# RWKV stage of a one-core block: heads of token half 1 turned one unit earlier, the next norm's weights in a place of their own, the fourth input unit in another PSUM bank

## The reference

```
x = layer_norm(ALPHA * x + 0.5 * swiglu_2(x, ...), ln_g[0, 0], ln_b[0, 0])      # norm "rw"
proj = x @ rwkv_w_in                                # 2816 columns = 11 units of 256
mix = rwkv7_mix(proj[..., :RWKV_SHIFT], ...)        # token shift, decays, chunked recurrence
heads = concatenate([mix, memory_attention(proj[..., RWKV_SHIFT:], mem_k, mem_v)])
x = layer_norm(ALPHA * x + heads @ w_out[0], ln_g[0, 1], ln_b[0, 1])            # norm "f4"
x = layer_norm(ALPHA * x + 0.5 * swiglu_2(x, ...), ln_g[0, 2], ln_b[0, 2])      # FFN 4

def layer_norm(x, g, b):
    mu = mean(x); var = mean((x - mu) ** 2)
    return (x - mu) * rsqrt(var + 1e-5) * g + b

# at the end of rwkv7_mix
    out = ((out - m) * rsqrt(var + 64e-5)) * lnx_g + lnx_b
    y = (out + bonus) * g
```

## Time and profile before

| | us |
|---|---|
| median of 3 runs | 1703.74 (1703.65 to 1704.11) |
| the profiled execution | 1700.73 |
| its span | 1699.4 |
| PE busy | 1639.3 (96%) |
| DVE busy | 942.3 (55%) |
| ACT busy | 802.6 (47%) |
| POOL busy | 129.6 (8%) |

### The profile page before, as it was taken

How to read it: one execution, slowest core, us unless ns; L and a number is a source line. 1 busy time by engine, 2 the same in 40 slices (tenths; PEclk the granted TensorE clock), 3 DMA queues, 4 the chain that set the end, 5 groups by cost and what they waited for, 6 DMA issues and landing times.

```text
span 1699.4 us, 29823 instructions
## 1 busy us (share of the span) xinstructions
PE 1639.3 (96%) x13094; PEld 1503.6 (88%) x13094; DVE 942.3 (55%) x1199; ACT 802.6 (47%) x1059; POOL 129.6 (8%) x117
## 2 busy tenths in 40 slices
PE   7999999988999999999999989999999999999998
PEld 7999897767999989998998879998999988789997
DVE  6444463445545555445795565546645474575545
ACT  6444444434444454444655254444544456764443
POOL 0000020000000001000376101000020010001000
PEclk9999999879999999999999999999999999999999
DMA  7745443313655445554530066454655542345551
GB/s 275 270 176 195 153 174 150 123 50 125 215 185 188 169 169 203 183 189 149 179 124 4 3 223 223 174 198 149 225 179 193 180 169 98 125 174 199 191 181 75
DMA packets 40865, 280.67 MB, mean 165 GB/s; under 512 B 4794, under 2 KB 4794, under 8 KB 8864
## 3 DMA queue, kind: packets, MB, share of 16 engines
q1 hardware_dynamic: 39024, 272.40, 44.6%
q0 software_dynamic: 1712, 6.37, 1.0%
HBM read 277.14 MB, written 1.08 MB: 164 GB/s over the span
## 4 chain that ended last, share of the span: by engine, by line
PE 90%; DVE 4%; ACT 3%; DMA 2%; issue 1%; SPq 0%; DVEq 0%; ACTq 0%
PE P L231 88%; PE P L242 2%; DMA raw<-ws 1%; ACT whi L205 1%; DMA gb<-gains 1%; DVE wlo L219 1%; DVE xt L279 1%; ACT xt L272 0%; DVE x L359 0%; PE P L2011 0%; DVE AR L791 0%; ACT AR L817 0%; DVE AR L371 0%; DVE AR L1077 0%; DVE AR L2120 0%
## 5 line engine op out<-in xcount | busy, mean ns | idle before, releaser
L231 PE MATMUL P<-xt,whi 128*128 128x256 f32 x5088 | 934.5, 286 | 14.6 <-DVE xt L279 12.1
L231 PEld LDWEIGHTS P<-xt,whi 128*128 128x128 f32 x5088 | 803.8, 193 | 29.3 <-issue 18.3
L231 PE MATMUL P<-xt,wlo 128*128 128x256 f32 x2544 | 702.3, 283 | 0.0
L219 DVE TENSOR_TENSOR wlo<-raw,whi 128x2048 fp32r<-128x2048 f32 x245 | 559.7, 2290 | 80.8 <-PE P L231 76.9
L205 ACT ACTIVATE whi<-raw 128x2048 fp32r<-128x2048 f32 x245 | 467.1, 1908 | 161.2 <-PE P L231 120.2
L231 PEld LDWEIGHTS P<-xt,wlo 128*128 128x128 f32 x2544 | 488.7, 192 | 0.0
L653 DVE TENSOR_TENSOR AR<-P,AR 128x256 f32<-128x256 f32 x114 | 48.4, 425 | 334.6 <-ACT AR L624 334.6
L624 ACT ACTIVATE AR<-P 128x256 f32<-128x256 f32 x114 | 43.7, 384 | 354.3 <-PE P L231 354.3
L231 PE MATMUL P<-whi,hh 128*128 128x512 f32 x504 | 197.5, 392 | 0.0
L231 PE MATMUL P<-wlo,hh 128*128 128x512 f32 x504 | 196.8, 390 | 0.0
L231 PE MATMUL P<-whi,hl 128*128 128x512 f32 x504 | 196.1, 389 | 0.0
(11 more groups left out here) (225 smaller groups left out, 934.8 us busy)
## 6 DMA issues: line engine op xcount, KB each, us to landing
raw<-ws SPq DMA_DIRECT2D x249, 1024.0 KB, 4.8
gb<-gains SPq DMA_DIRECT2D x16, 512.0 KB, 7.3
AR<-by_distance POOLq DMA_DIRECT2D x1, 3072.0 KB, 19.5
x<-x_in SPq DMA_DIRECT2D x2, 512.0 KB, 4.0
AR<-mem_in POOLq DMA_DIRECT2D x1, 1024.0 KB, 5.2
out<-x SPq DMA_DIRECT2D x2, 512.0 KB, 2.6
cs<-cst SPq DMA_DIRECT2D x1, 737.0 KB, 14.1
AR<-cst POOLq DMA_DIRECT2D x1, 420.0 KB, 4.6
```

Of the source, the lines that this page charges most:

```text
L219: dve.e.tensor_tensor(k.wlo[n % NLO][:, :], k.raw[u % NRAW][:, :], k.whi[n % NHI][:, :].bitcast(F32), ALU.subtract).then_inc(*k.s_lo.inc(u))
L231: return pe.e.matmul(o, l, r, start=start, stop=stop, skip_group_check=True)
```

## The change

It does five things.

1. `RW_PROJ`: unit U+3 goes to bank 6 instead of 3, U+5 to bank 7, U+6 to bank 6. PE's wait for `s_tt` of the lead unit U+1 ahead of U+3 goes. The waits of two bonus sums swap with their banks.
2. ACT's splits of the next units in the lead (`hi_to`) stand behind the cross copy of the next lead unit instead of ahead of it.
3. `heads_tensor(1)` stands ahead of half 0 of the third unit (U+14) instead of behind it.
4. The gains of norm f4 go to 2048 columns of the big work tile AR from column 3072 (the token-wise v and k of the stage lay there), and their load waits for `s_pe "read" 1`, the last reading of these, instead of for the heads.
5. SP's order around F0 is: gains, F1, F0, F2 instead of F0, gains, F1, F2.

```
+def gains_tile(k, name):
+    return ar(k, 3072, 2048, "p (a n) -> p a n", a=2) if name == "f4" else k.gb

 def load_gains(k, q, name, rows):
-        q.e.dma_start(k.gb[:, j, :], src).then_inc(*k.s_gn[j].inc(name, by=16))
+        q.e.dma_start(gains_tile(k, name)[:, j, :], src).then_inc(*k.s_gn[j].inc(name, by=16))

 (LayerNorm.rest_vector: in1=k.gb[:, 0, c] and k.gb[:, 1, c] become gains_tile(k, t)[:, 0, c] and [:, 1, c])

-RW_PROJ = {..., 3: (3, "LT", 18), 4: (0, "R", 0), 5: (6, "R", 2),
-           6: (7, "R", 4), ...}
+RW_PROJ = {..., 3: (6, "LT", 18), 4: (0, "R", 0), 5: (7, "R", 2),
+           6: (6, "R", 4), ...}

 (rwkv_inputs_tensor)
-    pe.wait_ge(*k.s_tt.after("rw", 1, 1))
-    cols_tensor(k, pe, U + 3, 3)
+    cols_tensor(k, pe, U + 3, 6)
...
-    cols_tensor(k, pe, U + 5, 6)
+    cols_tensor(k, pe, U + 5, 7)
     low_rank(1)
-    cols_tensor(k, pe, U + 6, 7)
+    cols_tensor(k, pe, U + 6, 6)

 (rwkv_inputs_scalar)
     for n in range(3):
         lead_scalar(k, act, "rw", U + n, n, k.rw_cross[n])
+        hi_to(k, act, U + n + 3)
         shifted_scalar(k, act, n)
         squares(2 * n)
         squares(2 * n + 1)
-        hi_to(k, act, U + n + 4)
+    hi_to(k, act, U + 6)

 (bonus_tensor)
-    pe.wait_ge(*(k.s_ev.after("kk", 5), k.s_ev.after("z", 3), k.s_ev.after("z", 5))[n])
+    pe.wait_ge(*(k.s_ev.after("kk", 5), k.s_ev.after("z", 5), k.s_ev.after("z", 3))[n])

 (rwkv_out_tensor)
     for u, n in units:
+        if n == 2:
+            heads_tensor(k, pe, 1)
         last = out_tensor(k, pe, u, n, False, 0)
     last.then_inc(*k.s_dn.inc("rw", "out"))
-    heads_tensor(k, pe, 1)

 (sync_program)
-    load_units(k, sp, U_FFN3 + 6, U_RWKV + 16)
-    gains("f4", (6, 7), [k.s_ev.after("heads", 1, 1)])
-    load_units(k, sp, U_RWKV + 16, U_FFN4 + 6)
+    load_units(k, sp, U_FFN3 + 6, U_RWKV + 15)
+    gains("f4", (6, 7), [k.s_pe.after("read", 1)])
+    load_units(k, sp, U_RWKV + 16, U_RWKV + 17)
+    load_units(k, sp, U_RWKV + 15, U_RWKV + 16)
+    load_units(k, sp, U_RWKV + 17, U_FFN4 + 6)
```

More of the change, by code:

```diff
@@ L371, in rest_vector @@
             dve.e.scalar_tensor_tensor(out=k.XC[:, a, c], in0=k.x[:, a, c], scalar=sm[:, 8 + a:9 + a],
-                                       in1=k.gb[:, 0, c], op0=ALU.add, op1=ALU.mult).then_inc(*k.s_dv.inc(t, "centred", a, h))
+                                       in1=gains_tile(k, t)[:, 0, c], op0=ALU.add, op1=ALU.mult).then_inc(*k.s_dv.inc(t, "centred", a, h))
         dve.wait_ge(*k.s_sq.after(t, a))
@@ L382, in rest_vector @@
             dve.e.scalar_tensor_tensor(out=k.x[:, a, c], in0=k.XC[:, a, c], scalar=sm[:, 10 + a:11 + a],
-                                       in1=k.gb[:, 1, c], op0=ALU.mult, op1=ALU.add).then_inc(*k.s_xn.inc(t, a, h))
+                                       in1=gains_tile(k, t)[:, 1, c], op0=ALU.mult, op1=ALU.add).then_inc(*k.s_xn.inc(t, a, h))
     def scalar(self, act, a):
@@ L1447, in wide @@
     return t.unsqueeze(2).to_broadcast([128, 12, 64])
-RW_PROJ = {0: (0, "K", 6), 1: (1, "K", 8), 2: (2, "K", 10), 3: (3, "LT", 18), 4: (0, "R", 0), 5: (6, "R", 2),
-           6: (7, "R", 4), 7: (0, "VT", 12), 8: (1, "VT", 14), 9: (2, "VT", 16)}
+RW_PROJ = {0: (0, "K", 6), 1: (1, "K", 8), 2: (2, "K", 10), 3: (6, "LT", 18), 4: (0, "R", 0), 5: (7, "R", 2),
+           6: (6, "R", 4), 7: (0, "VT", 12), 8: (1, "VT", 14), 9: (2, "VT", 16)}
 LOW_BANKS, BONUS_BANKS, QUERY_BANK = (4, 5), (3, 6, 7), 5
```

## The result

| | before | after |
|---|---|---|
| median of the timed runs, us | 1703.32 (20 runs, 1699.96 to 1707.33) | 1698.0 (20 runs, 1693.17 to 1703.08) |
| ratio of the times | | 0.9971 [0.9963, 0.998] |
| the profiled execution, us | 1700.73 | 1699.7 |
| its span, us | 1699.4 | 1698.4 |

The change makes the kernel faster by 0.29%: by the ratio 4.9 us, by its interval 3.4 to 6.3. Forecast were 1700.3 us and a gain of 3.47. The sign was right. The size was too small.

What follows compares the result with a forecast made beforehand. PE, busy 96% of the span, was taken as the bound, losing time only standing still or at half clock. Gains of 0.32 + 2.7 + 0.45 = 3.47 us took 1703.74 to 1700.3 us, range 1698.4 to 1702.2.

Steps and rivals of the forecast that it cites:

- rival D: Slower through PE's clock: extra half-clock bursts in input units, FFN 4's lead and long products, 1707.7 us; chance 0.03.
- Rival C: Moving half 1's heads does not reach norm f4, F0 lands no sooner: only 0.8 us gained, 1702.9 us; chance 0.08.
- The dip in half 1: Half clock within half 1 after PE stood 3.11 us: should vanish, counting for nothing in the sum.
- The dip in the lead: Half clock in F0's lead ahead of FFN 4, on the path: kept at its price of 1.5 us.
- rival B: The dip in FFN 4's lead grows: 1.5 us given back, 2.0 us gain remains, 1701.7 us; chance 0.19.
- Rival A: The dip ahead of FFN 4 goes or falls into PE's gap: 5.0 us gained in all, 1698.7 us; chance 0.20.
- The price of 1.5 us: Cost of half clock in F0's lead: 28 matmuls took 5.10 us there, 3.61 us at full clock.

Runs made afterwards that it cites:

- the filling: Full change plus three matmuls on constants, result overwritten, in PE's stand ahead of FFN 4's lead: 1696.35 us, ratio to the kernel before 0.9948.
- L388 first: Full change with ACT's split of F0 in norm f4 moved behind L388 of half 0: 1695.1 us, ratio 0.9943; run again 1693.54 us, 0.9948.

## Why the prediction was right and where it was not

**Edits 1 and 2: the term that failed.** The forecast was "Gain 0.32 us, and not more, since PE then ran without a stop for 59.84 us", with bounds of 0 and 0.32. The wait and its cause were read rightly. Two things were not.

First, the 0.32 is the idle time from the modelled end of one matmul to the start of the next. PE's start times say 0.47 and 0.64 in the two profiles of before shown above, and at equal clock (with a dip on both sides) the stage falls from 74.63 to 74.80 down to 74.04 to 74.14, that is by 0.5 to 0.75 us.

Second, "PE then ran without a stop" holds, but it ran a part of it at half clock. The dip near 840 us costs 1.5 us (74.1 against 72.56). It stands in all six profiles of kernels without edits 1 and 2, and in three of the ten with one or both. I had the dips on either side of the norm in my sum and looked for none here; the price was in no bound of the range either. Only rival D named dips in the input units, and as a loss.

Is that chance? The bare count is weak: the thought came up after six of these profiles, and of the ten taken later the dip is in three of three without the edits and in two of seven with them, which chance alone gives in 21 of 252 ways. The clock earlier in the same execution says more. Here are two profiles of one and the same kernel, the full change. The third of them, without a dip near 840, has one near 611 us, where nothing is edited; the first, with a dip near 840, has none there (windows, columns as above):

```profile
611.30:614.70 3.40, 3.40 (x18) 3.40 (x18) 0.08 (x1) 1.20 (x1) 0.00 (x0) 0.51 0.04 14
```

```profile
608.00:620.00 12.00, 9.78 (x81) 9.37 (x80) 3.01 (x6) 6.38 (x7) 0.00 (x0) 1.00 0.45 169
```

Sorted by that dip, all sixteen profiles fall into place. In the eleven that have it, the dip near 840 stands in four of four without edits 1 and 2 and in none of seven with one or both (chance: 1 in 330 ways). In the five that don't have it, the dip near 840 is always there, with the edits (three) and without (two). Read so, the edits take the dip away in the executions of the first kind and do nothing to it in the second. If eleven in sixteen is the share of the first kind, that is 0.7 dips an execution, 1.05 us, and the whole term is about 1.6. The sorting was found by looking at these same traces, and no run was made to try it.

The timed runs neither show this size nor rule it out. Edits 1 and 2 together have 1.0 us by the ratio, edit 1 alone -0.2 and edit 2 alone 0.5, each with an interval 3 to 4 us wide; the mean granted clocks of their runs, 0.9794, 0.9793 and 0.9794, against 0.9787, 0.9795 and 0.9795 in their runs of before, show no common rise.

Why the edits change the clock stays open. The matmuls in front of the dip are the same, with the same beat. In before they read:

```profile
836.24 2.85 PE L231 MATMUL P<-AR 12*128 12x256 f32 x12
839.03 1.14 PE L231 MATMUL P<-AR,gb 64*128 64x256 f32 x8
```

and the edits only bring them half a microsecond forward. No run took these thin matmuls away or filled them up.

**Edit 3** was right: forecast 2.7 us, and the stage fell by 2.70 to 2.75 in each of the eight profiles with it. PE's gap ahead of half 1 was to shrink from 3.11 to about 0.4 and is 0.38. The transposes were forecast near 975.3 and stand at 976.77, which is no fault of the term: the second reading was 1.18 us later in this execution. The claim that the path over F0 moves along also holds. Behind the second reading the split of F0 starts 19.12 us later in after and 21.91 in before, 2.8 us less. Rival C (the move doesn't reach the norm, 1702.9) falls with that, and with edit 3 alone measured at 2.9 us.

**Edits 4 and 5** were right: L374 waits for L388 instead of L371, the stage falls by 0.5 us (three profiles of before and those with other edits 12.9 to 13.5, six with the gains in their own place 12.55 to 12.73), where the forecast was 0.45. The 6.53 us of DMA in the chain were worth about a twelfth of their length, since the path over F0 ended only 0.5 us sooner. The gains, issued at 965.27, are waited for by nothing.

**The clock.** The dip in half 1 was to go at no gain, and it went: the windows 978 to 992 are at 1.00, and half 1's first matmul (980.70) and the next turn (988.99) lie 8.29 us apart, forecast 8.2. Over all profiles half 1 has half clock in the eight without edit 3, where PE stood 3.11 or 3.12 us ahead of it, and in none of the eight with it, where it stood 0.38.

The dip in the lead was kept, and two of three profiles of the full change have it as before (6.07, 6.05; 6.06 before). The stand ahead of it was forecast as 4 us and is 2.85 against 2.01. The profiled execution after has the longer dip, 6.90. That is rival B for one execution, with 0.84 of its 1.5 us. Rival A (the dip goes, 1698.7) is near the measured median, and would be the wrong reason for it: no profile of the full change lacks the dip. It took the filling, or L388 first, to remove it there.

The price of 1.5 us was read wrongly for the kernel before. Its second profile has no half clock in the lead, and from the first L359 of norm f4 to the second turn it takes 19.26 us, against 19.20 and 18.96 with it: without the dip PE stands for the norm of half 1. In the changed kernel that norm is done sooner, and there the dip is paid for: 18.61 and 18.72 us with it (19.57 with the longer one), 17.31 in the filled kernel. The sum, which kept the dip on both sides, isn't touched by this.

The Trainium skill ("TensorE: Matmul & The Clock Gate", section "HAM oscillation" in Part 1) says that a stand between bursts brings the half clock. By that the stand is to be filled or shortened, and here the runs agree: with a stand of 0.27 us the dip is gone, and with one of 1.07 us too, in the kernel with L388 first. The other profiles go the same way: ahead of the lead PE stood 2.01 to 2.85 us in the nine with half clock in it, and 1.07 to 1.46 us in the four unfilled others (in three of these half 1 had ended later, with twice as long a half clock in it, and in the kernel of edits 4 and 5 the lead began sooner). Rival D (slower by more dips) found nothing for it.

**The sum.** The chain of PE alone was forecast from 998.8 us on; it begins at 998.27 and 998.79 in two profiles of the full change, and at 1001.07 in the profile after, where the second reading came 1.2 us later and the lead took 0.8 longer. At equal clock it is 0.6 + 2.7 + 0.5 = 3.8 us instead of 3.47. With about 1.0 for the rarer dip, which is an estimate, it is 4.8 to 4.9; the ratio says 4.9, with an interval of 3.4 to 6.3. So the forecast gain of 3.47 lies within the interval, at its edge; that more than 3.8 was gained rests on all three measurements of the full change, 4.9, 4.4 and 6.3 us. Of the 2.3 us between 1700.3 and 1698.0, 0.4 is the reference (1703.74 from 3 runs, 1703.32 from 20), 0.3 to 0.4 are the terms at equal clock, about 1.0 is put down to the dip, and the remaining half a microsecond is less than what medians of 20 runs spread over 10 us can fix.

## What to carry to other kernels

Price a wait of PE by the step between start times less the beat, and look for stretches of half clock in all of the stage behind it, not only where PE stands: a change that shifts the stage can bring one or take it away, and each is worth about three times the wait here. Before a stretch of half clock gets a price, read what PE would wait for next without it. A transfer in the chain is worth only what lies between its end and the end of the next path, which must be named and read before the transfer is moved. And compare two profiles stage by stage, each as a difference of start times within one trace; total times of single executions differ by more than such a change gives.

## What the runs showed of the hardware

- **Half clock without a stand of PE.** Near 840 us PE is busy 4.00 of 4.00 us and gets 0.57; at 915 us, in one profile, 7.00 of 7.00 us and 0.52. Ahead of the first lie 12 matmuls with an output of 12 x 256 in 2.85 us and 8 with one of 64 x 256; a busy share of 100% in the records is no proof that the full clock is granted.
- **Work that isn't needed can pay.** Six matmuls of 2.74 us on constants, put in a stand of 2.85, kept the clock at 2.4 GHz in the one profile taken and made the burst behind them 1.5 us shorter (5.11 to 3.62 for 28).
- **A short stand and a long one.** Of the sixteen leads of FFN 4, the nine behind a stand of PE of 2.01 to 2.85 us have half clock in them, the seven behind one of 0.27 to 1.46 us have none.
- **Executions scatter by pieces that can be found.** The 11 to 35 runs of one kernel in one series lie within 4 to 13 us, but for two executions of before, of 2657.8 and 5512.76 us, which are left out of the ratios. In the profiles the unedited stage from the memory queries to the second reading varies from 82.56 to 86.96 us, and the one of norm sb, equally unedited, from 111.9 to 116.3, while FFN 4 to FFN 6 take 178.55 to 178.84 us in all of them.
